# A decoder trunk's compressed branch: first product in four column groups, first row maxima amid the index maxima, one split moved to GpSimd

## What is computed

```python
def _compress(tok, pe, w1, w2):
    ...
    blk = tok[:, idx] + pe[:, None, :]
    blk = jnp.swapaxes(blk, 2, 3).reshape(B, n_c, G, CMP_LEN * D)
    return jax.nn.gelu(blk @ w1) @ w2
```

## Time and profile before

| what | value |
|---|---|
| median of 3 runs | 1243.32 us (1243.03 to 1244.64) |
| the profiled execution's own time | 1243.99 us |
| its span | 1242.2 us |
| TensorE busy | 1211.8 us (98%) |
| VectorE busy | 554.5 us (45%) |
| ScalarE busy | 342.9 us (28%) |
| GpSimd busy | 121.7 us (10%) |
| HBM read | 452.26 MB, 365 GB/s over the span |

### The profile page before, as it was taken

The page is one execution under the profiler, slowest core; times in us unless marked ns, Lnnn a source line. Parts: engine busy times, 40 slices in busy tenths (PEclk is TensorE's granted clock), DMA queues, the critical chain, the costliest instruction groups (busy, mean ns, idle before and its releaser), DMA issues.

```text
span 1242.2 us, 25271 instructions
## 1 busy us (share of the span) xinstructions
PE 1211.8 (98%) x10409; PEld 632.6 (51%) x10411; DVE 554.5 (45%) x1549; ACT 342.9 (28%) x705; POOL 121.7 (10%) x165
## 2 busy tenths in 40 slices
PE   9998999999999999999999989999999999999995
PEld 8885754334444333443389858433433444443341
DVE  5788553333333333333368876433333333333334
ACT  4667321111111111111256574111111111111111
POOL 2661110000000000000035521000000000000000
PEclk9999999999999999999999999999999999999998
DMA  9544699999999999999945538999999999999994
GB/s 358 174 178 196 256 389 426 425 428 426 426 425 426 426 427 426 425 428 425 383 156 200 206 134 352 391 427 425 425 427 426 425 426 426 427 426 425 425 427 196
DMA packets 42425, 454.88 MB, mean 366 GB/s; under 512 B 4944, under 2 KB 5712, under 8 KB 8016
## 3 DMA queue, kind: packets, MB, share of 16 engines
q1 hardware_dynamic: 42032, 452.27, 87.8%
q10 hardware_dynamic: 288, 1.05, 0.2%
HBM read 452.26 MB, written 1.05 MB: 365 GB/s over the span
## 4 chain that ended last, share of the span: by engine, by line
PE 81%; DVE 9%; DMA 5%; ACT 3%; issue 2%; DVEq 0%; ACTq 0%; POOL 0%; POOLq 0%
PE banks L1039 33%; PE banks L1059 17%; PE banks L1015 7%; PE banks L1070 5%; DMA expert_weights<-in_moe_w 5%; ACT prob L1296 2%; PE banks L1047 2%; PE banks L959 1%; PE banks L906 1%; PE banks L907 1%; PE banks L908 1%; PE banks L626 1%; PE banks L594 1%; PE banks L996 1%; PE banks L596 1%
## 5 line engine op out<-in xcount | busy, mean ns | idle before, releaser
L1039 PE MATMUL banks<-expert_weights,gathered 128*64 128x512 f32 x1520 | 339.8, 595 | 1.9 <-DMA expert_weights<-in_moe_w 1.9
L1039 PEld LDWEIGHTS banks<-expert_weights,gathered 128*64 128x64 f32 x1520 | 105.6, 137 | 231.2 <-issue 231.2
L1059 PE MATMUL banks<-expert_weights,hT 128*32 128x512 f32 x1600 | 182.0, 595 | 2.5 <-DVE hT L1872 2.5
L1867 DVE TENSOR_TENSOR sig<-sig,banks 128x256 f32<-128x256 f32 x64 | 26.9, 421 | 339.3 <-ACT sig L1411 339.0
L1424 ACT ACTIVATE y_hi<-banks,gate_slot 128x512 fp32r<-128x512 f32 x126 | 86.6, 687 | 295.1 <-PE banks L1059 295.1
L1877 DVE SCALAR_TENSOR_TENSOR y_lo<-banks,gate_slot,y_hi 128x512 fp32r<-128x512 f32 x126 | 94.6, 751 | 157.6 <-ACT y_hi L1424 157.6
L1411 ACT ACTIVATE sig<-banks 128x256 f32<-128x256 f32 x64 | 24.6, 384 | 408.1 <-PE banks L1039 408.1
L1015 PEld LDWEIGHTS banks<-hot,x_part 128*128 128x128 bf16 x3072 | 93.3, 98 | 48.7 <-issue 48.7
L1059 PEld LDWEIGHTS banks<-expert_weights,hT 128*32 128x32 f32 x1600 | 47.5, 109 | 109.4 <-issue 107.9
L1015 PE MATMUL banks<-hot,x_part 128*128 128x64 bf16 x3072 | 100.6, 193 | 0.0
L1477 POOL TENSOR_TENSOR piece_lo<-piece,piece_hi 128x256 fp32r<-128x256 f32 x112 | 88.0, 824 | 78.9 <-ACT piece_hi L1236 63.3
(11 more groups left out here) (241 smaller groups left out, 1529.5 us busy)
## 6 DMA issues: line engine op xcount, KB each, us to landing
expert_weights<-in_moe_w SPq DMA_DIRECT2D x132, 2048.0 KB, 23.4
expert_weights_in_ring<-in_moe_w SPq DMA_DIRECT2D x20, 2048.0 KB, 23.4
piece<-in_pieces SPq DMA_DIRECT2D x32, 1024.0 KB, 5.0
expert_weights<-in_moe_w SPq DMA_DIRECT2D x26, 1024.0 KB, 8.7
expert_weights_in_rows<-in_moe_w SPq DMA_DIRECT2D x22, 1024.0 KB, 22.7
expert_weights_in_x<-in_moe_w SPq DMA_DIRECT2D x22, 1024.0 KB, 23.4
expert_weights_in_ring<-in_moe_w SPq DMA_DIRECT2D x8, 1024.0 KB, 8.7
shared_weights<-in_ws SPq DMA_DIRECT2D x2, 3072.0 KB, 12.1
```

The costliest lines, as they stand in the source:

```text
L1039: mm = pe.matmul(C[e * PAIR:(e + 1) * PAIR, :], xgT[:, d, e * PAIR:(e + 1) * PAIR], w[e][:, part], start=(d == 0), stop=(d == KD - 1))
L1059: mm = pe.matmul((A, B)[c][to:to + SLOTS, :], hT[:, f, of_:of_ + SLOTS], W[QUARTERS + c][e][:, f * 512:(f + 1) * 512], start=(f == 0), sto ...
```

## The change

Four things are done.

1. `cmp_hidden` sums the first 8 pairs of tokens in PSUM partitions 0 to 63 and the last 8 in 64 to 127, so four groups of 32 columns are used in turn. ScalarE copies the 128 rows to SBUF. A new step of TensorE, `cmp_sum`, adds the two halves by two matmuls with the two halves of the identity's columns, between the two tiles of `project(7)`. The gelu waits for that.
2. `maxima(0)` is done inside `index_top`, ahead of the sixth of the eight rounds over 256 columns.
3. ScalarE does `exps(0)` ahead of `split_hi(11)`. Where `split_hi(11)` stood, an exponential of one column is computed whose result nobody reads, and behind it stands the new copy.
4. The low part of piece 6 goes from VectorE to GpSimd.

```diff
-LO_VECTOR = (2, 3, 6, 14, 15, 16)
+LO_VECTOR = (2, 3, 14, 15, 16)
...
-        hgelu = place("hgelu", [2 * CROWS, 3, P])
+        hgelu = place("hgelu", [P, 3, P])
...
+        hid_sb, hid_sum = sem("cmp_hidden_halves_sb", 1), sem("cmp_hidden_summed", 1)
...
-                        for i in range(CPAIRS):
-                            for kv in range(2):
-                                n = STREAM.index(("cmp", kv))
-                                w1 = piece[n % RING][:, :, :].rearrange("p k c -> p (k c)")
-                                mm = pe.matmul(bank[7][kv * CROWS:(kv + 1) * CROWS, 0:P], blkT[:, kv, i, :], w1[:, i * P:(i + 1) * P],
-                                               start=(i == 0), stop=(i == CPAIRS - 1))
+                        each = CPAIRS // 2
+                        for i in range(each):
+                            for half in range(2):
+                                for kv in range(2):
+                                    n = STREAM.index(("cmp", kv))
+                                    w1 = piece[n % RING][:, :, :].rearrange("p k c -> p (k c)")
+                                    to, j = (2 * half + kv) * CROWS, half * each + i
+                                    mm = pe.matmul(bank[7][to:to + CROWS, 0:P], blkT[:, kv, j, :], w1[:, j * P:(j + 1) * P],
+                                                   start=(i == 0), stop=(i == each - 1))
                         mm.then_inc(hid, 1)
+
+                    def cmp_sum():
+
+                        pe.wait_ge(*at(hid_sb, 1))
+                        for half in range(2):
+                            mm = pe.matmul(bank[7][0:2 * CROWS, 0:P], ident[:, half * 2 * CROWS:(half + 1) * 2 * CROWS], hgelu[:, 2, :],
+                                           start=(half == 0), stop=(half == 1))
+                        mm.then_inc(hid_sum, 1)
...
-                    project(7)
+                    project_tile(7, 0)
+                    cmp_sum()
+                    project_tile(7, 1)
                     scores(1)
...
                     split_hi(10)
                     read_plain(6)
-                    split_hi(11)
+                    act.activation(ln_s[:, 0, 22:23], own_number[:, 0:1], ACT.Exp, scale=-1.0)
...
+                    act.wait_ge(*at(hid, 1))
+                    act.copy(hgelu[:, 2, :], bank[7][:, 0:P]).then_inc(hid_sb, 1)
                     exps(0)
+                    split_hi(11)
                     split_hi(12)
...
-                            for _ in range(TOPK // 8):
+                            for i in range(TOPK // 8):
+                                if a and i == 5:
+                                    maxima(0)
                                 own.link(V.max(top8[:, :], s))
                                 own.link(V.match_replace(s, top8[:, :], s, TAKEN))
...
                     misc()
-                    split_lo(6)
                     index_sum(0)
...
                     index_top()
-                    maxima(0)
                     rotate(7, (0,))
                     normalise(0)
-                    dve.wait_ge(*at(hid, 1))
-                    hx, hu, ho = (hgelu[:, j, :] for j in range(3))
+                    dve.wait_ge(*at(hid_sum, 1))
+                    hx, hu, ho = (hgelu[0:2 * CROWS, j, :] for j in range(3))
```

More of the change, by code:

```diff
@@ L683, in cmp_hidden @@
                         pe.wait_ge(*at(blk_ready, 2))
-                        for i in range(CPAIRS):
-                            for kv in range(2):
-                                n = STREAM.index(("cmp", kv))
-                                w1 = piece[n % RING][:, :, :].rearrange("p k c -> p (k c)")
-                                mm = pe.matmul(bank[7][kv * CROWS:(kv + 1) * CROWS, 0:P], blkT[:, kv, i, :], w1[:, i * P:(i + 1) * P],
-                                               start=(i == 0), stop=(i == CPAIRS - 1))
-                        mm.then_inc(hid, 1)
+                        each = CPAIRS // 2
[7 more added lines that the diff above has]
+                                                   start=(i == 0), stop=(i == each - 1))
+                        mm.then_inc(hid, 1)
+                    def cmp_sum():
[4 more added lines that the diff above has]
+                        mm.then_inc(hid_sum, 1)
                     def cmp_turn():
                         pe.wait_ge(*at(gelu_ready, 1))
-                        pe.transpose(bank[7][:, P:P + 2 * CROWS], hgelu[:, 2, :], ident[0:2 * CROWS, 0:2 * CROWS]).then_inc(hg_ps, 1)
+                        pe.transpose(bank[7][:, P:P + 2 * CROWS], hgelu[0:2 * CROWS, 2, :], ident[0:2 * CROWS, 0:2 * CROWS]).then_inc(hg_ps, 1)
                     def cmp_kv():
@@ L1323, in _ @@
                     act.wait_ge(*at(gelu_u, 1))
-                    act.activation(hgelu[:, 1, :], hgelu[:, 1, :], ACT.Exp, scale=1.0).then_inc(gelu_e, 1)
+                    act.activation(hgelu[0:2 * CROWS, 1, :], hgelu[0:2 * CROWS, 1, :], ACT.Exp, scale=1.0).then_inc(gelu_e, 1)
                     split_hi(SPLIT_OUT[0])
```

## The result

| | before | after |
|---|---|---|
| median | 1243.32 us (7 runs beside the change, 1242.84 to 1244.64) | 1248.42 us (7 runs, 1247.42 to 1253.08) |
| ratio to before, 95% interval | | 1.0040 (1.0029 to 1.0050) |
| the profiled execution | 1243.99 us, span 1242.2 | 1247.42 us, span 1245.5 |

The change makes the kernel 5.1 us slower. I had forecast 1240.2 us and given slower 3 in 100. In the profiled execution after, the first projection starts 0.91 us later than before. So for layer 1 I take 0.91 off every time of after that I compare.

The account below looks back on a forecast made before the run. VectorE in layer 1 and TensorE in layer 2 were taken as nearly even bounds, meeting at unit 0's turning. Layer 1's -2.0 and layer 2's -1.1 gave -3.1: 1240.2 us against 1243.32, range 1238.4 to 1242.6.

Parts of the forecast that it names:

- The product in four groups: TensorE's compressed product: 64 records in 16 rounds take 1.87 us instead of 3.61, 1.74 less per layer.
- The sum: TensorE, between project(7)'s tiles: two new float32 matmuls add 0.6 us (0.4 to 0.9), wholly on its path.
- The waits for part 5 and for the exponentials: TensorE in layer 1: waits of 0.52 at project(5) and 0.37 for the exponentials disappear.
- The rival that four groups don't overlap: Compressed product: 3.61 stays and the added 0.60 comes on top, giving 1243.7 us; chance 0.09.
- The low part of piece 6: Moved to GpSimd at no cost; VectorE gives up 2.66 us, index maxima come 2.1 (layer 1) and 0.9 (layer 2) earlier.
- ScalarE's order: High part 11 behind the exponentials; GpSimd's part 11 ends near 69.3, wanted at 75; costed at nothing.
- First maxima moved: VectorE in index_top: no wait in layer 1, ready at 65.8 before TensorE's 66.1; waits 0.9 in layer 2.
- Layer 2: Turning of unit 0 there: -1.74 + 0.60 = -1.1 us; VectorE's own gain is eaten by its wait.
- Sum: Unit 0's turning: -2.0 in layer 1 with VectorE ready at or before that, -1.1 in layer 2, together -3.1 us.
- A new wait takes part of it: Rival: GpSimd late with part 6, or VectorE's layer 2 wait delays normalising; about 1241.7 us, chance 0.15.
- The last 0.04: Chance left for one half-clock stretch more than now: +1.76 and a lost gain, about 1245 us or over.
- tied the clock to one wait: Rival: layer 1's half-clock stretch after the 1.17 wait for rotation goes, saving 1.76; 1238.5 us, chance 0.17.

Follow-up runs that it names:

- e2: The kernel before with only the low part of piece 6 moved to GpSimd; 1242.73 us, ratio 1.0001 (0.9988 to 1.0013).
- e9: The change with high part 11 ahead of the first exponentials again, part 6 still on GpSimd; 1243.67 us, ratio 1.0001 (0.9992 to 1.0010).
- e3: The kernel before with only the product in four groups, ScalarE's copy and the sum; 1243.25 us, ratio 1.0000 (0.9987 to 1.0012).
- e4: The change with part 6 back on VectorE and high part 11 early again; 1244.09 us, ratio 0.9999 (0.9989 to 1.0009).
- e6: The change with part 6 on VectorE and GpSimd's part 11 held until the gelu's second stage; 1244.74 us, ratio 1.0008 (0.9998 to 1.0018).
- e15: The change with six of eight rounds of index maxima (mask keeps 48 keys, not 64); 1240.97 us, ratio 0.9980 (0.9971 to 0.9989).
- e8: The kernel before with five bf16 products of a zero tile ahead of piece 9's wait; 1242.96 us, ratio 0.9998 (0.9989 to 1.0008).
- e10: The kernel before with VectorE's subtraction for part 14 done later in two halves; 1244.08 us, ratio 1.0006 (0.9997 to 1.0015).
- e7: e6 with five bf16 products of a zero tile ahead of piece 9's wait; 1243.74 us, ratio 1.0002 (0.9993 to 1.0012).
- e11: e4 with VectorE's subtraction for part 14 done later in two halves; 1244.89 us, ratio 1.0011 (1.0002 to 1.0020).

## Why the prediction was wrong

**The product in four groups** (-1.74 per layer) and **The sum** (+0.6) were right: 3.61 became 1.88 and the sum is 0.65. The waits for part 5 and for the exponentials went as said. The rival that four groups don't overlap, and the Trainium skill's 81 ns per matmul (TensorE: Matmul & The Clock Gate) that I set beside it, fall: 64 records in 1.88 us are 29 ns each, 59 for a matmul of two records.

**The low part of piece 6** failed: "On GpSimd this costs nothing while this cover holds". I looked at when GpSimd would be done, and that held (part 6 ended at 46.7 - 0.9 = 45.8, wanted at 47.9). I did not ask whom it runs beside, though the earlier trace rows had the answer in 7.65 against 5.72, and I used those two numbers for GpSimd alone. VectorE's sums take twice their time beside part 6 (3.27 against 1.64 for four), and the index maxima come 0.8 us later, not 2.1 earlier. In the time this step cost little by itself (e2, e9); it ate the gain that the forecast had put in VectorE.

The Trainium skill bears on this (GPSIMD Engine Reference, section 1, Specifications): GpSimd's SBUF interfaces are shared with VectorE, with contention for VectorE's instructions of two SBUF inputs or in a two-port mode. Perfetto Trace Analysis, section Optimizing Scalar/DVE Operations, adds that moving work between the two "might not help". The traces agree: the sums, with two tiles from SBUF, went from 0.35 to as much as 0.76 us each. The gelu's two steps of one input went from 0.22 to 0.64; whether they are in a two-port mode no row shows.

**ScalarE's order** failed most: "I cost this at nothing". I checked that part 11 would be in time for piece 9. I had it end near 69.3, so it would start near 63.5, on just the stretch in which VectorE rotates and normalises unit 0 and starts the gelu. It started at 66.74 - 0.91 = 65.8, 2.3 later than that, but VectorE was late as well, and it found the same steps. It cost 0.5 us on the add and 1.3 on the gelu; normalising (1.64) had been slow before too (1.56, against 1.03 with nothing beside it). Undone alone (e9), it takes the loss of 4.9 us with it.

**First maxima moved** was right in the order of things (no wait at them in layer 1). The wait of 0.9 forecast for layer 2 didn't come, since VectorE reached the maxima late, at 678.01. In layer 1 VectorE was to be ready at 65.8 and was at 68.8 (69.75 - 0.91). Of these 3.0 us, 2.9 are the index maxima being 0.8 later where I had 2.1 earlier. What part 11 added there, my allowance of 3.5 us from the maxima to the hand-over nearly held. Its 1.3 us on the gelu come behind that and make unit 1 late.

**Layer 2** was forecast 1.1 us shorter up to the turning of unit 0. That came at 686.24 against 684.66, 1.6 later, which is just how much later the layer began: nothing won. The index maxima there were to be 0.9 earlier and are 1.1 later (666.81 - 1.61 against 664.09).

**Sum.** "VectorE is ready at or before that" is the sentence that fell. TensorE's 1.1 to 2.0 us stood at a meeting point where VectorE was the later one. e3, e4 and e9 show the consequence without any loss: with the product 1.73 us shorter in each layer they are even with before. What is won ahead of unit 0 is waited for at unit 0 (e9, 1.86) or at piece 9 (e6, 2.14; e15, 1.07). Even with six rounds, the change was only 1.0 us better than the kernel before with six (1240.97 against 1242.00), and the intervals of the two overlap.

**The rivals.** *A new wait takes part of it* had the right kind of mechanism and the wrong place and size: I had it on GpSimd's lateness. The last 0.04 (a half-clock stretch more) is part of what happened: 10.5 us at 1.2 GHz in the mixers instead of 3.5, less 1.7 us of it in which TensorE waited anyway, is worth (an estimate) 2.6 us of TensorE's time in the profiled execution. I had tied the clock to one wait and gave no thought to a wait of 3 us elsewhere bringing its own stretch.

Shown by runs: the late part 11 carries the loss; 2.6 us of slack on VectorE remove it. Not shown by an experiment: how the loss divides between slower instructions and half-clock stretches. These come and go (in the mixers' profiles none in e2, e8 and e10, one before, a long and a short one after), and no run held the clock up behind the wait of 2.98. But every run's mean granted clock is on record: 0.991 to 0.995 for the change, 0.9930 on average, against 0.9953 to 0.9960 for the kernel before in the four groups of some 30 runs beside the experiments. The difference times 1246 us is 2.9 to 3.7 us of clock, waits included. So by this estimate the clock may be more than half of the 5.1 us.

None of the 13 kernels that compute everything that the reference asks for is faster than the kernel before by more than the measurement tells.

## What to carry to other kernels

When work moves to GpSimd, or moves in time on it, list VectorE's instructions beside it. Price each short one with a wait for a slice (here up to 0.7 us, which made arithmetic on SBUF tiles take two to three times as long), and each long one as a wait of GpSimd's. Then ask which engine is the later one at the next meeting point. A gain on the other is nothing there, and a loss on the later one brings its clock's cost with it. A cheap test of which it is: shorten the suspected engine's work in both kernels, and compare; then look whether the collisions are still where they were, since in e15 two of them had gone.

## What the runs showed of the hardware that I had not expected

- Beside a GpSimd subtraction of 128x256 slices, VectorE's instructions of SBUF tiles slow down unequally: the sum of 128x128 from 0.35 to 0.76 us, that of 128x256 from 0.48 to 0.95, a tensor_scalar of 64x128 from 0.22 to 0.64. They end 0.1 to 0.3 us behind the slice that they met. The rotation's products, which read PSUM, kept their 0.42, and the index maxima kept 0.43 a piece.
- GpSimd loses little to short instructions and much to a long one: eight slices took 5.58 us alone, 6.33 beside the index sums, and 7.65 beside VectorE's one subtraction of 2.66.
- A half-clock stretch of some 3.5 us followed a wait of 1.17 us (before, at piece 9), and one of 7 us began within a wait of 2.98. Products of a zero tile in the wait at piece 9 raised the mean granted clock over ten runs from 0.9946 (e6) to 0.9969 (e7).
- The first projection starts from 0.36 us earlier (e2) to 1.14 later (e11) than in the profiled execution of before, as much as one part of this change was to win.
